# A pad in the constants shortened by 32 bytes: the matmul operands and the work buffers change halves of a 64-byte line

## The reference

```python
def _swiglu(x, w_gu, w_down):
    g, u = jnp.split(x @ w_gu, 2, axis=-1)
    return (jax.nn.silu(g) * u) @ w_down

for layer in range(DEPTH):
    x = x + 0.5 * _swiglu(_rms_norm(x, ffn1_norm[layer]), ...)   # 1024 -> 2 x 2816 -> 1024
    h = _rms_norm(x, mix_norm[layer])
    x = x + mixer(h)
    x = x + 0.5 * _swiglu(_rms_norm(x, ffn2_norm[layer]), ...)
```

## The kernel before, in words

| buffer | before | modulo 64 | after | modulo 64 |
|---|---|---|---|---|
| raw, high, low, levels, prm, cst | 1152 to 77248 | 0 | the same | 0 |
| picks | 84608 | 0 | 84576 | 32 |
| x | 86688 | 32 | 86656 | 0 |
| xs (matmul operand) | 94880 | 32 | 94848 | 0 |
| gs, sg | 111264, 113312 | 32 | 111232, 113280 | 0 |
| ends (matmul operand) | 115360 | 32 | 115328 | 0 |
| rstd | 131744 | 32 | 131712 | 0 |
| var, guess, newt | 132800, 134848, 136896 | 0 | 32 less each | 32 |
| small, work, roots | 140352, 140608, 222528 | 0 | 32 less each | 32 |

## Time and profile before

### The profile page before, as it was taken

The page is one execution under the profiler, slowest core; times in us unless marked ns, Lnnn a source line. Parts: engine busy times, 40 slices in busy tenths (PEclk is TensorE's granted clock), DMA queues, the critical chain, the costliest instruction groups (busy, mean ns, idle before and its releaser), DMA issues.

```text
span 3370.9 us, 59401 instructions
## 1 busy us (share of the span) xinstructions
PE 3316.9 (98%) x23740; PEld 3079.6 (91%) x23740; DVE 2595.7 (77%) x3030; ACT 1650.9 (49%) x1753; POOL 203.6 (6%) x158
## 2 busy tenths in 40 slices
PE   8999999999999999999999999999999999999999
PEld 8999899998899998699999989999999999999998
DVE  7779777777777777577877977777898777789876
ACT  4464545445545444454546444544555454455544
POOL 0100000110000000000000000000170000017000
PEclk9999999999999999899999999999999999999999
DMA  7553366554355554145555335455544545554454
GB/s 265 187 188 113 128 212 200 203 191 153 113 198 178 198 187 153 61 178 191 187 191 189 114 125 200 175 200 187 188 166 170 203 174 200 187 185 167 168 205 163
DMA packets 98937, 593.01 MB, mean 176 GB/s; under 512 B 25684, under 2 KB 26836, under 8 KB 27736
## 3 DMA queue, kind: packets, MB, share of 16 engines
q1 hardware_dynamic: 97280, 586.47, 48.6%
q10 hardware_dynamic: 1496, 4.20, 0.3%
HBM read 588.53 MB, written 2.11 MB: 175 GB/s over the span
## 4 chain that ended last, share of the span: by engine, by line
PE 92%; DVE 6%; ACT 1%; issue 1%; DMA 0%; DVEq 0%; SPq 0%; ACTq 0%
PE wide L580 26%; PE wide L581 14%; PE wide L451 8%; PE wide L453 8%; PE wide L452 8%; PE acc L451 7%; PE acc L453 7%; PE acc L452 7%; DVE low L1855 1%; PE acc L757 1%; PE wide L875 0%; PE acc L682 0%; PE acc L762 0%; ACT high L1315 0%; PE wide L693 0%
## 5 line engine op out<-in xcount | busy, mean ns | idle before, releaser
L1855 DVE TENSOR_TENSOR low<-raw,high 128x2048 fp32r<-128x2048 f32 x531 | 1218.2, 2297 | 223.7 <-ACT high L1315 221.6
L1315 ACT ACTIVATE high<-raw 128x2048 fp32r<-128x2048 f32 x550 | 1049.3, 1910 | 609.6 <-PE acc L453 366.3
L580 PE MATMUL wide<-xs,high 128*128 128x512 f32 x3840 | 1337.4, 390 | 0.1
L581 PE MATMUL wide<-xs,low 128*128 128x256 f32 x3840 | 1082.8, 282 | 0.0
L580 PEld LDWEIGHTS wide<-xs,high 128*128 128x128 f32 x3840 | 720.6, 188 | 148.5 <-issue 1.2
L581 PEld LDWEIGHTS wide<-xs,low 128*128 128x128 f32 x3840 | 725.8, 189 | 0.0
L451 PE MATMUL acc<-ends,high 128*128 128x256 f32 x2192 | 611.6, 279 | 0.0
L452 PE MATMUL acc<-ends,high 128*128 128x256 f32 x2192 | 611.1, 279 | 0.0
L453 PE MATMUL acc<-ends,low 128*128 128x256 f32 x2192 | 611.1, 279 | 0.0
L451 PE MATMUL wide<-xs,high 128*128 128x256 f32 x1912 | 543.6, 284 | 14.2 <-DVE low L1870 12.1
L452 PE MATMUL wide<-xs,high 128*128 128x256 f32 x1912 | 534.6, 280 | 0.0
(11 more groups left out here) (252 smaller groups left out, 3433.2 us busy)
## 6 DMA issues: line engine op xcount, KB each, us to landing
raw<-stream SPq DMA_DIRECT2D x550, 1024.0 KB, 4.8
work<-rpb SPq DMA_DIRECT2D x16, 256.0 KB, 6.3
work<-bias_shifted ACTq DMA_DIRECT2D x2, 1024.0 KB, 4.7
work<-start SPq DMA_DIRECT2D x1, 1218.0 KB, 15.4
x<-x_in SPq DMA_DIRECT2D x1, 1024.0 KB, 5.0
raw<-stream SPq DMA_DIRECT2D x2, 512.0 KB, 7.0
work<-bias_by_distance ACTq DMA_DIRECT2D x2, 512.0 KB, 5.6
bias_shifted<-work ACTq DMA_DIRECT2D x1, 1024.0 KB, 3.9
```

What stands on the lines that cost most here:

```text
L580: nc.tensor.matmul(out[:, n, :, :], wh, xs[:, :, k, :], start=(k == 0), stop=False, skip_group_check=True)
L581: last = nc.tensor.matmul(out[:, n, 0, :], wl, xh[:, k, :], start=False, stop=(k == KC - 1), skip_group_check=True)
L1315: nc.scalar.activation(high[:, s % HIGH, :], raw[:, s % RAW, :], ACT.Copy).then_inc(high_ready, 1)
L1855: v.tensor_tensor(low[:, s % LOW, :], raw[:, s % RAW, :], high[:, s % HIGH, :].bitcast(F32), ALU.subtract).then_inc(low_ready, 1)
```

## The change

One number: the unused field at the end of the constants is 152 floats wide where it was 160. The constants' transfer becomes 128 x 1832 floats instead of 128 x 1840, and every buffer behind `cst` begins 32 bytes lower, as in the table above. No instruction on any engine is added, removed or moved; only addresses differ.

```diff
@@ _consts
     for name, width in (
         [("ident", P), ("ones", P), ("heads", 70), ("whole", 70), ("ropes", 68), ("rot", P)]
-        + [("cos", T), ("sin", T), ("namask", GRID_W), ("fxmask", TT * T), ("pad", 160)]
+        + [("cos", T), ("sin", T), ("namask", GRID_W), ("fxmask", TT * T), ("pad", 152)]
     ):
```

## The result

Slower, by 1.8%. The changed kernel takes 3432.53 us (median of four runs, 3430.07 to 3433.25), the kernel before 3371.4 us in the same session: the ratio is 1.0177, with a 95% interval of 1.0164 to 1.0189. That is 61 us more, and outside the forecast range. The profiled execution took 3432.01 us, its span 3430.2.

What follows compares the result with a forecast made beforehand. TensorE's steps were taken to bound the kernel, gate and `three` making 2950 us of the 3371 us span. Every term of the change was taken as 0 or cancelling, giving an unchanged 3371.5 us, range 3365 to 3378.

Steps and rivals of the forecast that it cites:

- Gate and `three`: TensorE's two big matmul streams: steps of three stay at 116.7 ns with both operands aligned, 0 us change.
- First reading: Token-major matmuls, weights moving from a multiple of 64: 173.1 ns per 384 columns, the gate's surplus despite an aligned moving operand.
- Second reading: Matmuls on roots and picks, both operands on multiples of 64: 0.113 us a step, nearer 116.7 ns than 107.
- Third and fourth reading: Plain float32 sums on work: 0.213 us a step, no surplus; ends at half clock: 0.2125 us, no odd-start price.
- The work side: Plain float32 matmuls, VectorE and ScalarE on buffers going off the line: taken as 0, plain matmuls at most 29 us.
- The slower rival: Moving and stationary rows starting in the same half of a 64-byte line slow both streams: 28 us, 3400 us; chance 0.14.
- The rule of 187 us: Skill formula N / 2.4 + 2.5 ns per warm matmul: if odd starts explained the excess, a 187 us drop to 3185 us.
- What bounds the kernel: TensorE, busy 98% of the span; other engines wait for it, so time is the sum of its steps.

Runs made afterwards that it cites:

- c: Kernel before with 32 spare bytes ahead of high: weights on odd multiples of 32 bytes, xs and ends on multiples of 64; 3372.27 us, ratio 1.0000.
- d: Changed kernel, weights, xs, ends all on odd multiples of 32 bytes: 3432.77 us. In "d = 0", d is bytes modulo 512 from weight tile to moving row.
- b: Kernel before with 32 spare bytes ahead of rstd, so only the work buffers behind ends move; 3372.15 us, ratio 1.0001.
- a: Changed kernel with 32 spare bytes ahead of rstd, so rstd, var, newt, work and roots return to their old places; 3432.44 us, ratio 1.0178.
- g: Kernel before with the pad at 168 floats instead of 160, xs and ends 64 bytes from the weights modulo 512; 3406.79 us, ratio 1.0109.
- h: Changed kernel with xs and ends begun 16 bytes into longer buffers, xs at distance 16 and ends at 80; 3446.74 us, ratio 1.0224.
- m: Kernel before with the pad at 184 floats instead of 160, xs and ends 128 bytes from the weights modulo 512; 3412.51 us, ratio 1.0118.
- f: Kernel before with the pad at 144 floats instead of 160, xs and ends 480 bytes from the weights modulo 512; 3412.69 us, ratio 1.0120.
- l: Kernel before with the pad at 176 floats instead of 160, xs and ends 96 bytes from the weights modulo 512; 3425.26 us, ratio 1.0151.
- i: Changed kernel with xs and ends begun 48 bytes into longer buffers, xs at distance 48 and ends at 112; 3374.61 us, ratio 1.0004.
- u: Changed kernel with 4608 down-projection steps loading 64 of 128 weight columns, output's upper half getting nothing from them; 3405.37 us, ratio 1.0093.
- e: Changed kernel with 32 spare bytes ahead of low: moving rows at distance 32 from high and 0 from low; 3374.23 us, ratio 1.0006.
- p: Kernel before with 480 spare bytes ahead of low: moving rows at distance 0 from high and 32 from low; 3410.36 us, ratio 1.0116.
- t: Kernel before with 4608 down-projection steps loading 64 of 128 weight columns, output's upper half getting nothing from them; 3384.18 us, ratio 1.0032.
- k: Changed kernel with 32 spare bytes ahead of ends: xs at distance 0, ends where it was before, at 32; 3394.86 us, ratio 1.0067.

## Why the prediction was wrong

**The step that failed** is in "Gate and `three`": "I take 116.7, the value of both aligned-moving and unaligned-moving rows: 0 us." It is 61.3 us by the balance above, of which the token-major matmuls gave 1.9 back. I asked where an operand begins relative to a line, and found the same price for rows on and off it. The variable was the distance of the two operands, and c and d show that: same distance, same time, wherever they begin.

- **First reading.** The earlier trace rows looked like the two arrangements to compare. Both have their operands 32 bytes apart, the one with the activations above, the other below. They could not show what another distance costs. After the change has its answer here, at distance 0 with the weights moving:

```profile
2440.85 0.33 PE L451 MATMUL wide<-high,xs 128*128 128x384 f32 x1
...
2447.95 0.34 PE L453 MATMUL wide<-high,xs 128*128 128x384 f32 x1
```

  41 steps in 7.10 us are 173.2 ns, against 173.1. With the weights moving, the same shift changed nothing in the 384-column stream.
- **Second reading.** The earlier trace rows stood for "both on the line". Its operands are 192 bytes apart modulo 512, a distance of its own, and as both moved by 32 bytes it has not changed: the row after is 0.62 us again. It was no evidence on d = 0.
- **Third and fourth reading.** Their durations held, and they misled. Plain float32 sums take 1.02 us after as before. That row was misread in its count: a plain float32 matmul leaves two records (L495 on `newt` has 36, for 18 normalisations), so its four records are two sums, each of four passes of 107 ns; the 0.213 us is the price of one record. At half clock the step after is that of the earlier trace rows:

```profile
1364.92 0.41 PE L452 MATMUL wide<-ends,high 128*128 128x256 f32 x1
...
1366.84 0.41 PE L452 MATMUL wide<-ends,high 128*128 128x256 f32 x1
```

  1.92 us over 9 steps are 213.3 ns, at granted clock 0.50 and d = 0. "The surplus belongs to the full clock and to this number type" is thus borne out. What I added, that where the row begins is not needed to explain it, was right for one operand and wrong for two.
- **The work side.** The zeros for plain float32 (0.03 us in 1756 records), VectorE and ScalarE held; b shows it alone. The 7 ns between `gs` and `newt` did not swap, so they are not a matter of the line.
- **The slower rival** had the right place, moving row against weights, and the right sign. Its price was too small: 28 us against 61.3. I took 1.1 ns a step from the earlier trace rows; on the mean over the trace a step is 3.2 ns longer on `ends` into `acc` and 2.5 on `xs`, and the pair lost 6.2 where I gave it 3.3. Its rule, both starts in the same half of a line, has the sign right in a to d and in g, h and m; f and l contradict it, and so does i in its gate pair. I held against it, which is the misreading above, and gave it 0.14.
- **The rule of 187 us.** The Trainium skill, "TensorE: Matmul & The Clock Gate", section "Back-to-back issue gap", gives the formula that I used for an isolated matmul, and these streams have a weight load for each. No arrangement tried came near its 109.2 ns: the shortest step in a feed-forward loop is 113.5 ns, in u.
- **What bounds the kernel** held: the time moved with TensorE's steps and no wait came or went.

What stays open: why a step takes more than its columns at full clock only, which distances are good and why, which of the two weight tiles holds a step (e and p fit neither reading), whether the load or the written output makes the difference in t and u, and what puts a stream into one rhythm or the other.

## What to carry to other kernels

A layout change that shifts one matmul operand against the other can move every step of a kernel that TensorE bounds, here from 1.0224 down to 0.9948 of the time, so after any change of a buffer or a pad look at the start-to-start step of the main streams first. Before arguing from two rows that an address does not matter, work out for both rows the difference of the operands' addresses, and not only where each begins. If steps carry a surplus over their columns, try some offsets of the moving operands on the chip, each stream by itself and then together, since no rule found here predicts the good ones, and k shows that the place of one stream's operand can change another stream's time.

## What the runs showed of the hardware

- A 256-column step of reduced float32 with its own weight load took from 113.5 to 120.0 ns at full clock, for 106.7 ns of columns at 2.4 GHz; only addresses and, in t and u, the width of the load and of the output differed. At half clock it took its columns, 213 ns, at d = 32 and at d = 0.
- Identical instructions at identical addresses ran at 346.9 or 353.4 ns a pair within one trace, each over a whole stretch of 32 pairs.
- Halving the columns of the weight load, and with them the rows of the output, made the step 6.3 ns shorter at d = 0 and 2.3 ns longer at d = 32.
- Shifts by 32 bytes left plain float32 matmuls (0.213 us a record of 256 columns), ScalarE (599 ns) and VectorE (690 ns) as they were.
